# Hybrid decoder trunk, one core: the last four weight slabs bank by bank, the final norm by statistics instructions, and RWKV and mLSTM pieces placed elsewhere

## What is computed

```
p = x @ w_in                                  # 2048 x 6412
o_rw  = RWKV-7 time mixing of p[:, :1792]     # 8 heads of 64
o_ret = silu(g) * rms(retention(...))         # 6 heads of 128
o_ml  = sigmoid(o) * (rms(mLSTM(...)) * ml_norm)   # 6 heads of 128
x1 = layernorm(ALPHA * x + [o_rw|o_ret|o_ml] @ w_out)
x2 = layernorm(ALPHA * x1 + (silu(x1 @ w_gate) * (x1 @ w_up)) @ w_down)
```

## Time and profile before

| | |
|---|---|
| median of 3 runs | 2814.73 us (2813.31 to 2817.98) |
| the profiled execution | 2812.47 us, of which its span 2810.6 us |
| mean granted TensorE clock | 0.988 |
| PE busy (matmul) | 2718.1 us, 97% |
| DVE, ACT busy | 58%, 42% |
| HBM traffic | 158 GB/s over the span |

### The profile page before, as it was taken

The page is one execution under the profiler, slowest core; times in us unless marked ns, Lnnn a source line. Parts: engine busy times, 40 slices in busy tenths (PEclk is TensorE's granted clock), DMA queues, the critical chain, the costliest instruction groups (busy, mean ns, idle before and its releaser), DMA issues.

```text
span 2810.6 us, 55797 instructions
## 1 busy us (share of the span) xinstructions
PE 2718.1 (97%) x23575; PEld 2639.4 (94%) x23575; DVE 1629.6 (58%) x1770; ACT 1166.9 (42%) x1454; POOL 0.2 (0%) x4
## 2 busy tenths in 40 slices
PE   7998999999999999999999999998999999999996
PEld 7988889899999999999999989897999999999996
DVE  5566456688545445454586574576964545455445
ACT  4444334446333333333363453353653333333333
POOL 0000000000000000000000000000000000000000
PEclk9999999999999999999999999999999999999998
DMA  7543226255555555554565542253655555555552
GB/s 236 163 139 100 84 77 197 91 176 182 172 181 177 179 179 176 177 180 168 180 195 151 168 118 75 78 166 106 185 186 179 174 179 175 181 173 203 182 178 99
DMA packets 280504, 447.37 MB, mean 159 GB/s; under 512 B 45414, under 2 KB 76448, under 8 KB 280040
## 3 DMA queue, kind: packets, MB, share of 16 engines
q1 hardware_dynamic: 278712, 441.59, 50.1%
q10 hardware_dynamic: 1618, 3.21, 0.4%
HBM read 432.97 MB, written 11.78 MB: 158 GB/s over the span
## 4 chain that ended last, share of the span: by engine, by line
PE 89%; DVE 6%; ACT 3%; issue 1%; ACTq 0%; DVEq 0%
PE psum L699 20%; PE psum L700 20%; PE psum L698 20%; PE psum L731 6%; PE psum L732 6%; PE psum L733 6%; DVE w_lo L1734 2%; ACT w_hi L1305 1%; PE psum L721 1%; PE psum L723 1%; PE psum L722 1%; PE psum L928 1%; PE psum L1099 1%; PE psum L1084 1%; PE psum L1088 1%
## 5 line engine op out<-in xcount | busy, mean ns | idle before, releaser
L1730 DVE TENSOR_TENSOR w_lo<-w_raw,w_hi 128x1024 fp32r<-128x1024 f32 x496 | 605.7, 1225 | 695.7 <-ACT w_hi L1292 693.4
L1292 ACT ACTIVATE w_hi<-w_raw 128x1024 fp32r<-128x1024 f32 x504 | 533.9, 1061 | 909.9 <-PE psum L700 880.1
L698 PE MATMUL psum<-x_hi,w_lo 128*128 128x264 f32 (+3 forms) x3072 | 879.2, 286 | 1.9 <-DVE x_lo L2057 1.0
L700 PE MATMUL psum<-x_hi,w_hi 128*128 128x264 f32 (+3 forms) x3072 | 879.5, 286 | 0.0
L699 PE MATMUL psum<-x_lo,w_hi 128*128 128x264 f32 (+3 forms) x3072 | 878.8, 286 | 0.0
L698 PEld LDWEIGHTS psum<-x_hi,w_lo 128*128 128x128 f32 x3072 | 582.1, 189 | 3.1 <-issue 1.3
L699 PEld LDWEIGHTS psum<-x_lo,w_hi 128*128 128x128 f32 x3072 | 581.5, 189 | 0.2
L700 PEld LDWEIGHTS psum<-x_hi,w_hi 128*128 128x128 f32 x3072 | 580.4, 189 | 0.0
L1734 DVE TENSOR_TENSOR w_lo<-w_raw,w_hi 128x1024 fp32r<-128x1024 f32 x304 | 368.2, 1223 | 223.8 <-ACT w_hi L1305 207.1
L1305 ACT ACTIVATE w_hi<-w_raw 128x1024 fp32r<-128x1024 f32 x292 | 304.5, 1055 | 313.4 <-PE psum L733 236.4
L731 PE MATMUL psum<-x_hi,w_lo 128*128 128x264 f32 (+1 forms) x1376 | 412.5, 300 | 6.7 <-DVE w_lo L1734 3.8
(11 more groups left out here) (505 smaller groups left out, 2483.7 us busy)
## 6 DMA issues: line engine op xcount, KB each, us to landing
w_raw<-in_w_in SPq DMA_DIRECT2D x192, 512.0 KB, 3.6
w_raw<-in_w_gate SPq DMA_DIRECT2D x176, 512.0 KB, 3.5
w_raw<-in_w_up SPq DMA_DIRECT2D x176, 512.0 KB, 4.0
w_raw<-in_w_down SPq DMA_DIRECT2D x176, 512.0 KB, 4.2
w_raw<-in_w_out SPq DMA_DIRECT2D x64, 512.0 KB, 3.9
w_raw<-in_w_in SPq DMA_DIRECT2D x16, 262.0 KB, 2.8
r_sample<-in_state_ret SPq DMA_DIRECT2D x6, 512.0 KB, 8.3
out_s_ret<-r_sample SPq DMA_DIRECT2D x6, 512.0 KB, 6.2
```

The source lines that it names most:

```text
L698: mm(out, w1, bh[:, k, 0:nt], start=(k == 0), stop=False)
L700: last = mm(out, w0, bh[:, k, 0:nt], start=False, stop=(k == last_k))
L1292: A(wh[:, j, :, :], raw[:, j, :, :], ACT.Copy).then_inc(S.hi_ready, 1)
L1730: TT(wl[:, j, :, :], raw[:, j, :, :], wh[:, j, :, :].bitcast(F32), ALU.subtract).then_inc(S.lo_ready, 1)
```

## The change

1. The product loop on PE stops before the last four slabs. These are then done bank by bank: all 24 matmuls of the first column block over the four slabs, then those of the second, and so on. Each bank is added to the residual and transposed while PE does the next ones.
2. The final norm of the prompt takes mean and variance from `bn_stats` and `bn_aggr`, in place of two sums, squares on ACT and eight small operations.
3. The sample's last operations move ahead of prompt pieces 6 to 8, and its sixteen stores become one, placed after prompt piece 5.
4. RWKV plan: layer 0 `bonus` 15 to 24 tiles and `tok0` 34 to 37; layer 1 `tok0` 24 to 28 and `tok1` 10 to 12. All later pieces stand so many tiles later.
5. Two `bg.step()` stand inside `mix` of the value columns.
6. mLSTM: high parts of weights may be made between the gate activations.
7. The squares of the 256 prompt columns of `a_y` are made at `sy` and `syt`; only the 8 sample columns (`SEQ:T`) are left at the old place. This holds for retention and mLSTM.

```
-        [('in', 0), ('a', 7), ('g', 7), ('kk', 11), ('kks', 9), ('bonus', 15)] +
-        chunk_steps(0, 34) + chunk_steps(1, 10) + rw_last,
+        [('in', 0), ('a', 7), ('g', 7), ('kk', 11), ('kks', 9), ('bonus', 24)] +
+        chunk_steps(0, 37) + chunk_steps(1, 10) + rw_last,
         [('in', 0), ('a', 7), ('g', 7), ('kk', 11), ('kks', 9), ('v', 88), ('bonus', 6)] +
-        chunk_steps(0, 24) + chunk_steps(1, 10) + rw_last]
+        chunk_steps(0, 28) + chunk_steps(1, 12) + rw_last]
...
-                for b in range(KB):
-                    sp.dma_start(o['y_sample'][:, 0, 128 * b:128 * b + 128], ysm[NS * b:NS * b + NS, :]).then_inc(S.y_stored, 16)
+                    if 4 * t + q == 4:
+                        sp.wait_ge(S.ln_folded, 2 * DEPTH + 6)
+                        sp.dma_start(o['y_sample'][:, 0, :].rearrange("s (b c) -> b s c", c=128), ysm[:, :]).then_inc(S.y_stored, 16)
...
-            for j in range(4 * DOWN_SLABS):
+            for j in range(YB):
...
+            for n in range(4):
+                for j in range(YB, YB + 4):
+                    if n == 0:
+                        pe.wait_ge(S.lo_ready, s + j + 1)
+                    for h in range(2):
+                        k = 2 * (j % DOWN_SLABS) + h
+                        w0 = wh[:, j % RING, h, 128 * n:128 * n + 128]
+                        w1 = wl[:, j % RING, h, 128 * n:128 * n + 128]
+                        out = ps[:, 4 + n, 0:T]
+                        mm(out, w1, hh[:, k, 0:T], start=False, stop=False)
+                        mm(out, w0, hl[:, k, 0:T], start=False, stop=False)
+                        last = mm(out, w0, hh[:, k, 0:T], start=False, stop=(k == FB - 1))
+                last.then_inc(S.slab_used, 1)
+                if n:
+                    pe.wait_ge(S.ln_scaled, 10 * DEPTH + n)
+                    if n == 3:
+                        pe.wait_ge(S.y_rows, 4)
+                    turn(11 + n, 2 * ((n - 1) % 2), 1).then_inc(S.y_turned, 1)
+            pe.wait_ge(S.ln_scaled, 10 * DEPTH + 4)
+            pe.wait_ge(S.y_rows, 5)
+            turn(15, 2, 1).then_inc(S.y_turned, 1)
...
                 if ml:
                     A(pml[:, 12:16, 0:T], pml[:, 12:16, 0:T], ACT.Sigmoid)
+                    bg.to('score')
                     own(A(ptail[:, 0:2, 0:T], ptail[:, 0:2, 0:T], ACT.Sigmoid))
+                    bg.step()
+                    bg.step()
...
-                for name in tuple(f'v{p}' for p in range(AP_)) + ('sy', 'syt', 'sumsq'):
+                for name in tuple(f'v{p}' for p in range(AP_)) + ('sy',):
                     bg.to(name)
+                act.wait_ge(S.a_y_kept, 3 * n + 2)
+                A(sq[:, 0:3, 0:SEQ], ay[:, 0:3, 0:SEQ], ACT.Square)
+                bg.to('syt')
+                A(sq[:, 3:AH, 0:SEQ], ay[:, 3:AH, 0:SEQ], ACT.Square)
+                bg.to('sumsq')
                 act.wait_ge(S.a_y_ready, n + 1)
                 if ml:
-                    A(sq[:, :, :], ay[:, :, :], ACT.Square).then_inc(S.a_squares, 1)
+                    A(sq[:, :, SEQ:T], ay[:, :, SEQ:T], ACT.Square).then_inc(S.a_squares, 1)
...
                     for i in range(5):
                         mix(l, 8, 4, i)
+                        if i in (0, 3):
+                            bg.step()
...
+            for n in range(4):
+                dve.wait_ge(S.slab_used, s + YB + n + 1)
+                Rb = R[:, 12 + n, :]
+                TT(Rb, Rb, ps[:, 4 + n, 0:T], ALU.add).then_inc(S.ln_scaled, 1)
+            dve.wait_ge(S.ln_scaled, 10 * DEPTH + 4)
             v.tensor_copy(rsm[:, :].rearrange("p (b s) -> p b s", s=NS), R[:, :, SEQ:T]).then_inc(S.ln_scaled, 1)
...
+            dve.wait_ge(S.y_rows, 6)
+            for t in range(2):
+                v.bn_stats(yst[:, t, 18:24], Y[:, t, 3 * GC:3 * GC + 384])
+            dve.wait_ge(S.y_turned, 7)
+            own(v.tensor_copy(Y[:, 1, 3 * GC + 384:], ps[:, 3, 0:128]))
+            v.bn_stats(yst[:, 1, 24:30], Y[:, 1, 3 * GC + 384:])
+            dve.wait_ge(S.y_rows, 7)
+            own(v.bn_stats(yst[:, 0, 24:30], Y[:, 0, 3 * GC + 384:]))
+            for t in range(2):
+                last = v.bn_aggr(ymv[:, t, :], yst[:, t, :])
+            last.then_inc(S.ln_sum, 1)
+            dve.wait_ge(S.y_rows, 8)
             v.tensor_reduce(sm1, ysm[:, :], AX.X, ALU.add).then_inc(S.ln_sum, 1)
```

More of the change, by code:

```diff
@@ L301, in build @@
     rsm = at("y_sample_columns", P_END + 512, [128, 128])
[L302 to L308, removed]
+    ycol = at("y_columns", P_END + T * 4, [128, 40, 2])
+    yst = ycol[:, 0:30, :].rearrange("p a b -> p (a b)").rearrange("p (t k) -> p t k", t=2)
+    ymv, ysd, yroot = ycol[:, 30:32, :], ycol[:, 32, :], ycol[:, 33, :]
+    sm1, nms, sm2, sds = (ycol[:, 34 + i, 0:1] for i in range(4))
+    YB = 4 * DOWN_SLABS - 4
     x_tok = at("x_rows", 0, [128, 2, D])
@@ L1268, in _ @@
             pe.wait_ge(S.y_rows, 3)
[L1269 to L1274, removed]
+            for n in range(4):
[19 more added lines that the diff above has]
+            turn(15, 2, 1).then_inc(S.y_turned, 1)
+            pe.wait_ge(S.ln_scaled, 10 * DEPTH + 5)
+            pe.wait_ge(S.y_rows, 6)
+            tr(ps[:, 0, 128:256], rsm[:, :], ident).then_inc(S.y_turned, 1)
             pe.wait_ge(S.start_loaded, 96)
@@ L1414, in attention @@
                         last = A(g, g, ACT.Identity, scale=col(l, 'ml_norm', h), bias=eps[:, 3:4])
+                        if h in (1, 3):
+                            bg.step()
                     last.then_inc(S.a_gate, 1)
-                for name in ('score', 'num0', 'num1', 'vt'):
+                for name in ('score', 'num0', 'num1', 'vt')[1 if ml else 0:]:
                     bg.to(name)
@@ L2563, in _ @@
-            STT(yv, ss, 1.0 / D, yd, ALU.mult, ALU.subtract).then_inc(S.ln_sum, 1)
-            dve.wait_ge(S.y_rows, 5)
+                if k in (48, 68, 80):
+                    q = (48, 68, 80).index(k)
+                    dve.wait_ge(S.y_rows, q + 1)
+                    for t in range(2):
+                        v.bn_stats(yst[:, t, 6 * q:6 * q + 6], Y[:, t, GC * q:GC * q + GC])
+            for n in range(4):
+                dve.wait_ge(S.slab_used, s + YB + n + 1)
+                Rb = R[:, 12 + n, :]
+                TT(Rb, Rb, ps[:, 4 + n, 0:T], ALU.add).then_inc(S.ln_scaled, 1)
@@ L2572, in _ @@
                     y, g = Y[:, i // 4, GC * (i % 4):GC * (i % 4) + GC], gains[:, :, GC * (i % 4):GC * (i % 4) + GC]
-                    made = own.mark(STT(y, y, nmu[:, i // 4:i // 4 + 1], g[:, 0, :], ALU.add, ALU.mult))
+                    made = own.mark(STT(y, y, ymv[:, i // 4, 0:1], g[:, 0, :], ALU.subtract, ALU.mult))
                 if i:
```

90 lines of the change are left out of this document (23 added, 67 removed).

## The result

The changed kernel takes **2799.12 us**, median of 6 runs (2798.26 to 2802.41), the kernel before 2813.43 (6 runs beside it, 2812.04 to 2817.98): ratio 0.995, 95% interval 0.994 to 0.996. The forecast was 2797, its own range 2792 to 2801, 8 in 10 between 2789 and 2806. The profiled execution took 2799.05 us, its span is 2797.3: 13.3 less than before, where the sum said 17.8. Later, in another group of runs, five runs of the same file gave 2797.47 (ratio 0.9939, 0.9926 to 0.9953), which by that ratio is 17.2 less.

The account below looks back on a forecast made before the run. PE, on the chain for 89% of the span, was taken to bound the kernel. Terms -4.1 - 4.2 - 3.5 - 6.0 = -17.8 us gave span 2792.8, median 2797; own range 2792 to 2801, 8 in 10 2789 to 2806.

Parts of the forecast that it names:

- layer 0 RWKV: Layer 0 bonus and tok0: more tiles ahead shrink PE's stalls, less 0.3 lost at tile 112; -4.1 us.
- layer 1 RWKV: Layer 1: mix stall 2.3 gained, its half clock 1.7, other pieces and boundaries gain and lose; -4.2 us.
- squares, retention: Retention, both layers: PE's wait of 0.49 before the sum of squares goes; 2 x 0.5 us gained.
- squares, mLSTM: mLSTM, both layers: PE's wait of 2.11 before the sum falls by 1.3 each; clock bounds 0 and 1.7 each.
- high parts: mLSTM gates: one high part made 3 us sooner, no PE stall stands there; 0, at most 0.5 us lost.
- end: After slab 83: statistics instructions, earlier sample work and one sample store end the span sooner; -6.0 us, bounds -4.5 and -7.5.
- Tile 176 ... where ACT is free: its wait there was below 0.2, all gained: Layer 0, group boundary at tile 176: falls before more0's like in chunk 1, its wait below 0.2 us all gained.
- the walk: Layer 0, bonus to tok0: PE reaches tok0 0.35 us later with 12 tiles (4.5 us) more done; 4.2 gained.
- (b): Clock rival: half-clock stretches behind bonus, both sums of squares and mix go; -23 us, 2792, chance 0.16.
- (a): Rival: the stalls only move, so RWKV gives 0; -9.5 us, 2805, chance 0.23.
- (c): Rival: no change that can be told, RWKV costs 5 and the end gives 4; 2813, chance 0.07.
- (d): Slower rival: SP waits at layer 0 slab 88 for chunk 1's inverse, loads come late; 7 slower, 2822, chance 0.04.

Follow-up runs that it names:

- The one-tile run: The changed kernel with layer 0's tok1 9 tiles behind out0 in place of 10, so more1 ends its filler at tile 176: 2798.17 us, ratio 0.9939.
- The parts run alone: Three runs on the kernel before: RWKV plans with mix steps 2811.71 us, the new end 2808.14 us, the squares 2807.78 us.
- six tiles more: The tuned kernel with six more tiles ahead of tok0 in layer 0 and one more ahead of more0: 2795.6 us, ratio 0.9934.
- the second experiment: The changed kernel with RWKV plans set by DVE's goals: layer 0 tok0 36 for 37; layer 1 tok0 26 for 28, tok1 14 for 12: 2792.12 us.
- the tuned one: The changed kernel with both RWKV plans re-placed, among others layer 0 bonus 29, tok0 31 and layer 1 tok0 26, l0 5, tok1 13: 2793.17 us, ratio 0.9934.

## Why the prediction was right, and where it was not

**Total.** Right, and in part by luck: terms missed in both directions. In the first pair of profiles RWKV gave 3.3 for 8.3, the squares in mLSTM 4.4 for 2.6, those in retention 1.0, and the end 4.5 for 6.0, which is the 13.3 but for 0.1. What each stage took, from its own PE waits in the profiles, with forecasts beside:

| term | forecast | measured | from |
|---|---|---|---|
| layer 0 RWKV | -4.1 | -0.7 (mean -2.4) | 190 to 501: 311.4 before, 310.7 after, each with 14 us of half clock in it; means of 3 and 6 profiles with the old and new plan 312.5 and 310.0, with 18.3 and 12.0 us of half clock |
| layer 1 RWKV | -4.2 | -2.6 (mean -2.9) | 1570 to 1875: 307.97 before, 305.35 after; means of 3 and 6 profiles 308.1 and 305.2 |
| squares, retention | -1.0 | -1.0 | waits of 0.49 and 0.51 gone |
| squares, mLSTM | -2.6 | about -6 | 501 to 583 and 1875 to 1953: means of 3 profiles with 2.11, 81.2 and 81.7; of 10 with 0.83, 78.6 and 77.9 |
| high parts | 0 | none seen | ratio 0.994 without them, 0.9939 with them |
| end | -6.0 | -6.0 | 158.3 and 152.3, clocks alike |

The parts run alone give by their ratios -3.4, -8.2 and -5.6, together -17.2, where the whole gave 14.1 in its first runs and 17.2 in its later ones; each is uncertain by 2.5 to 3.1.

**Layer 0 RWKV: the step that failed** is "Tile 176 ... where ACT is free: its wait there was below 0.2, all gained". Up to `tok0` the walk held: the changed kernel starts it 0.24 earlier with 12 tiles (4.5 us) more done, and led by 0.4 at 190 already: 4.3 gained, 4.2 said. Then 0.3 went at tile 112 as said, and 2.11 less the 0.37 and 0.18 that stood there before went at `more1`. I had looked for who waits for a bank. I had not worked out DVE's goal at `more1`, which the tile past the boundary makes 24 (23 one tile sooner) and which so puts a second low part there (about 1.1 us), nor looked for who waits for the high part that ACT makes behind the banks (0.7). The half clock at 358.7 took up to 1.7 more. The one-tile run shows that the tile past the boundary is the cause; it also shows that the wait is not the whole loss. The larger gain of the mean, 2.4, goes with less half clock: behind `bonus` the three profiles with the old plan have 6.8 us of it each, those with the new one 0, 3.4 or 6.8.

**Layer 1 RWKV.** The stall and its clock went as said; the run without the steps shows both. The other items were near their sizes (`more0` 1.33 for 1.1, 1.34 less 0.40 for 0.85, 1.35 at tile 240 gone). What fell short is small and spread: 0.49 at 1818 and 0.87 at 1853 are new waits, not in the sum.

**Squares.** The wait fell to 0.83, as said (the sum of the recorded items is 3.6, carried as 3.5). The clock, which I left at bounds of 0 and 1.7 each, was the larger half: rival (b) held here, and behind `bonus` in two of the eight profiles with a wait of 2.96 there. Over all profiles, in the 5 us behind the sum the granted clock was 0.66 or 0.67 in 5 of 6 cases with a wait of 2.11 and 1.00 in all 20 with 0.83.

**The end.** Sum right, parts off: the last low part cost PE 0.27 (0.25 said), a `bn_stats` of 128 columns 0.29 for 0.2, yet from the start of the last addition to the first multiply-add it is 3.8 for 4.2, and landing took 2.7 for 2.4, so that the last multiply-add ended 3.1 before the end for 2.8 said. In the first pair of profiles 1.5 of it is masked by half clock behind the 2.65 us wait at 2645.

**Rivals.** (a) is half true of layer 0: waits moved and boundaries cost, but RWKV as a whole gave 3 to 5 us, not 0. (b) is half true, as said under the squares. (c) is out. (d) was not reached, and six tiles more reach it.

## What to carry to other kernels

When pieces of work are moved against a planned filler, recompute the goal of every engine at every piece, and look at each group boundary for a goal that jumps and for the copies that stand in front of the next operand, not only for the bank. In these runs a wait of 2.1 us or more in front of dense matmuls mostly cost up to 1.7 us again in clock, one of 0.8 nothing, so the long ones are often worth more than their length. It is no rule: 2.28 at `tok0` was followed by no half clock in five profiles of five, and half clock also came with no wait ahead of it (below). And where another engine's chain sets the time between two pieces, more filler does not move the second piece's start (19.12 and 19.11 us with 31 and 37 tiles), and lost clock moves it by less than it costs elsewhere (2.1 us for two stretches).

The best version found is the second experiment: 2792.12 us, 0.9917 (0.9903 to 0.993) of the kernel before. The intervals of the tuned one and of the changed kernel's later runs overlap it.

## What was not expected of the hardware

- Waits repeat between executions and chips to 0.02 us where the clock ahead of them is the same, stretches at half clock do not. With the same plan the wait at `tok0` was 2.28 where half clock stood behind `bonus`, and 3.07 where none did. Behind the 2.65 us wait of layer 1's down projection the clock fell in 11 of 13 profiles; behind 2.84 to 2.86 at 1650 in 4 of 4, behind 0.33 there in none of 9. Behind `bonus` no such stretch, one or two of 3.4 us followed 2.96, with the same waits ahead. The kernel before ran from 2808 to 2819 us at mean clocks of 0.990 to 0.986 (42 runs), 2.4 us for each 0.001. The Trainium skill (TensorE: Matmul & The Clock Gate, "Part 1: The HAM clock gate") says that the watching is free-running and that the same kernel shows different numbers of slow matmuls in different runs. The changed kernel's two profiles agree with the second; the first no run here can show.
- Half clock costs by what PE does in it. Between `bonus` and `tok0`, where DVE sets the pace, none made 19.1 us, one stretch of 3.4 us 19.9, two 21.2: 0.8 and 2.1, not 1.7 and 3.4.
- Half clock comes without a wait too. In both layers PE does 128 matmuls of one column in a row, near 430 and 1830, and in all 13 profiles, 26 places of 26, half clock begins inside them or up to 1.5 us behind, with no wait over 0.4 in the 8 us before. In the changed kernel it begins at 433.7 and lasts 6.8:

```profile
430.71 4.57 PE L1167 MATMUL psum<-p_rw,rw_sample 64*64 64x1 f32 x128
```

- How the chip chooses where the clock falls stays open here; it was not tried to hold it up by filling the waits.
